# A new beginning for a two-block transformer kernel: modulation vectors, squares and the first block of weights before the norm

## The chip, the cores and the metric

The kernel runs on one core of a Trainium2 chip. The metric is the device time in microseconds of one execution. It is given as the median of three runs. Five engines work side by side and meet through semaphores: TensorE (PE) does matmuls into PSUM, VectorE (DVE) and ScalarE (ACT) work element by element, GpSimd (POOL) does so without access to PSUM, and SyncE (SP) issues most transfers.

## The reference, cut to what matters

The program computes two blocks one after the other, for 512 positions of 1024 features. The first has two layers of three sublayers (gated FFN, mixer, gated FFN), the second is another mixer with an FFN. The change touches the beginning of the first sublayer:

```python
c_act = jax.nn.silu(c)
for l in range(DEPTH):
    mod = (c_act @ w_mod[l] + b_mod[l]).reshape(c.shape[0], N_MOD, D_MODEL)
    h = modulate(x, g_norm[l, 0], mod[:, 0], mod[:, 1])     # shift, scale
    x = x + 0.5 * mod[:, 2][:, None, :] * swiglu(h, w_ffn1_gu[l], w_ffn1_down[l])
...
def rmsnorm(x, g):
    y = x * lax.rsqrt(jnp.mean(x * x, axis=-1, keepdims=True) + EPS)
    return y * g
def modulate(x, g, shift, scale):
    return rmsnorm(x, g) * (1.0 + scale[:, None, :]) + shift[:, None, :]
```

So h = rstd * (x * a) + shift with a = (1 + scale) * g, where rstd belongs to a position and a and shift to a feature. A product with weights W is then rstd * ((x * a) W) + shift W, and (x * a) W can be had before rstd is known.

## The kernel before, in words

Features lie on the 128 partitions, in 8 chunks, and the 512 positions on the free axis. All weights come as blocks of 1 MB (1024 x 256) into four places of `raw`. ScalarE rounds each half of a block to `w_hi` (line 1179), GpSimd takes the rest `w_lo` (line 464), two places each. A product of a chunk is three fp32r matmuls for each of two column tiles: high by high, low by high, high by low (lines 551 to 553). One block is therefore 8 x 2 x 3 = 48 matmuls over 512 columns. Blocks alternate between PSUM banks 0, 1 and 2, 3; `out_free` says when the pair of banks has been taken.

At the beginning SP issues `cond` (208 KB), three tables `mod_b`, `gains`, `ident` (104, 40 and 64 KB), then x (2048 KB), then the first four "positions", which are vectors of 512 modulation values with 2048 KB of weights each, in four pieces of 512 KB. Positions 0 and 1 make the shift, 2 and 3 the scale. Block 0 of the weights is issued ahead of position 3, block 1 behind it.

Two engines compute the positions. For 0 and 2 TensorE multiplies the activated condition, repeated over 128 columns in `cond_wide`, with the weights: 8 fp32 matmuls (line 859), of two passes each. VectorE then picks the diagonal (line 1721). For 1 and 3 VectorE multiplies and adds eight times over 512 columns (lines 2427 and 2429), copies the partial sums to `t_ring`, and TensorE sums the partitions by products with a column of ones (line 866). ScalarE squares x chunk by chunk (line 1185), VectorE adds the squares up (line 1729), and TensorE sums them over the partitions (lines 589, 600). VectorE makes the variance (1743), GpSimd the power (469), TensorE spreads rstd over the partitions (608). Then `norm` makes h chunk by chunk: VectorE x * a * rstd into PSUM (1837), ScalarE adds the shift and rounds (1216), VectorE takes the low part (1834). Block 0 starts with the first chunk of h.

All later sublayers begin in another way. `ahead` on ScalarE scales x by a alone (lines 1193, 1194), VectorE takes the low part (`scaled_x`, 1775), and TensorE multiplies the sublayer's first block with it (634 to 636) while the squares are still being summed. VectorE sums the shift's product with that block from `raw` (`bias_sum`), and `scale_part` (1811, 1815) multiplies the result by rstd afterwards. The order in each engine's queue is the order in which the code is written; no scheduler changes it.

## Time and profile before

| | us |
|---|---|
| median of 3 runs | 2747.59 |
| lowest and highest | 2746.55, 2747.94 |
| span of the profiled execution | 2745.7 |
| TensorE busy | 2682.1 (98%) |
| VectorE busy | 1357.7 (49%) |
| ScalarE busy | 1070.1 (39%) |
| GpSimd busy | 1142.1 (42%) |

The profiled execution's own time is its span, 2745.7 us, with 1.9 us less than the median of the runs. Busy shares are an average over the whole program; the change lies in the first 80 us, so the views of that stretch say more. Starts are counted in microseconds from the span's start. A matmul's duration overlaps that of the next one, so its cost is read from the distance of starts. A fp32 matmul has two passes and two rows in the trace; a fp32r matmul has one.

### The profile page before, as it was taken

Reading aid. Unit: us, or ns where it says so; the run is one execution under the profiler, and the core shown is the slowest. Engines: PE = TensorE matmul, PEld = TensorE weight load, DVE = VectorE, ACT = ScalarE, POOL = GpSimd, SP = SyncE. Lnnn points to the kernel's source line nnn. Section 1 sums busy time; section 2 is a strip of 40 time slices with the busy share of each in tenths; the row PEclk is TensorE's granted clock in tenths of the full one; section 3 lists DMA queues with packets and bytes.
Section 4 is the critical chain, followed back from the end, with each engine's and each line's share of the span. In section 5 each row is a group of like instructions: output and inputs, shape, how many; then the busy total and the mean of one; then the engine's idle time right before and its main releaser. Section 6 shows DMA issues by size and latency. Waiting matters only on the chain.

```text
span 2745.7 us, 34606 instructions
## 1 busy us (share of the span) xinstructions
PE 2682.1 (98%) x12784; PEld 2181.2 (79%) x12784; DVE 1357.7 (49%) x2212; ACT 1070.1 (39%) x1600; POOL 1142.1 (42%) x492
## 2 busy tenths in 40 slices
PE   6999999999999999999999999999999999999998
PEld 4888887788888888888778888888766878888886
DVE  5333247763232543324776333345764557674645
ACT  3222245452222532224545222246465563542333
POOL 2444444144444444444424444455321334344343
PEclk9999999999999999999999999999999999999999
DMA  7545432146454264543214545434310214322231
GB/s 285 198 160 201 160 138 92 47 144 215 163 204 164 100 215 161 199 162 138 92 47 145 210 166 201 167 123 161 110 47 32 77 70 169 108 99 100 92 108 46
DMA packets 70723, 378.82 MB, mean 138 GB/s; under 512 B 7936, under 2 KB 8704, under 8 KB 40352
## 3 DMA queue, kind: packets, MB, share of 16 engines
q1 hardware_dynamic: 65568, 358.56, 36.5%
q10 hardware_dynamic: 4992, 18.09, 1.8%
q8 instruction: 101, 1.65, 0.2%
q14 instruction: 62, 0.51, 0.1%
HBM read 368.23 MB, written 8.39 MB: 137 GB/s over the span
## 4 chain that ended last, share of the span: by engine, by line
PE 79%; DVE 10%; DVEq 4%; ACT 3%; issue 2%; DMA 1%; ACTq 1%; SPq 1%; POOL 0%
PE psum L551 21%; PE psum L553 21%; PE psum L552 21%; PE psum L570 1%; PE psum L572 1%; PE psum L571 1%; DVE psum L1837 1%; PE psum L730 1%; PE psum L732 1%; PE psum L731 1%; PE psum L665 1%; PE psum L664 1%; PE psum L663 1%; DVEq L2270 1%; DVE small L2051 1%
## 5 line engine op out<-in xcount | busy, mean ns | idle before, releaser
L464 POOL TENSOR_TENSOR w_lo<-raw,w_hi 128x1024 fp32r<-128x1024 f32 x464 | 1119.3, 2418 | 1484.3 <-ACT w_hi L1179 1469.4
L1179 ACT CAST w_hi<-raw 128x1024 fp32r<-128x1024 f32 x464 | 483.1, 1047 | 822.6 <-PE psum L553 696.5
L551 PE MATMUL psum<-h_hi,w_hi 128*128 128x512 f32 x1920 | 750.4, 391 | 8.9 <-DVE h_lo L1834 5.2
L553 PE MATMUL psum<-h_hi,w_lo 128*128 128x512 f32 x1920 | 748.0, 390 | 0.0
L552 PE MATMUL psum<-h_lo,w_hi 128*128 128x512 f32 x1920 | 748.0, 390 | 0.0
L551 PEld LDWEIGHTS psum<-h_hi,w_hi 128*128 128x128 f32 x1920 | 361.1, 188 | 87.7 <-issue 7.2
L553 PEld LDWEIGHTS psum<-h_hi,w_lo 128*128 128x128 f32 x1920 | 361.0, 188 | 75.3
L552 PEld LDWEIGHTS psum<-h_lo,w_hi 128*128 128x128 f32 x1920 | 361.1, 188 | 75.0 <-issue 0.5
L1920 DVE TENSOR_TENSOR psum<-act_ring,psum 128x512 f32<-128x512 f32 x85 | 59.2, 696 | 517.8 <-ACT act_ring L1249 517.4
L551 PE MATMUL psum<-hid_hi,w_hi 128*128 128x512 f32 x792 | 308.5, 389 | 0.8 <-DVEq L1869 0.8
L553 PE MATMUL psum<-hid_hi,w_lo 128*128 128x512 f32 x792 | 308.1, 389 | 0.0
L552 PE MATMUL psum<-hid_lo,w_hi 128*128 128x512 f32 x792 | 308.1, 389 | 0.0
L1865 DVE SCALAR_TENSOR_TENSOR x<-psum,gate,x 128x512 f32<-128x512 f32 x128 | 90.3, 747 | 334.6 <-PE psum L553 300.1
L1710 DVE CUSTOM_DVE_ANT_0 mod_sink<-mod_raw,psum 128x1024 f32<-128x1024 f32 x192 | 234.1, 1220 | 37.8 <-issue 26.7
L1249 ACT ACTIVATE act_ring<-psum 128x512 f32<-128x512 f32 x85 | 50.8, 598 | 355.1 <-PE psum L553 355.1
L551 PEld LDWEIGHTS psum<-hid_hi,w_hi 128*128 128x128 f32 x792 | 148.7, 188 | 32.7 <-issue 2.0
L553 PEld LDWEIGHTS psum<-hid_hi,w_lo 128*128 128x128 f32 x792 | 148.7, 188 | 30.9
L552 PEld LDWEIGHTS psum<-hid_lo,w_hi 128*128 128x128 f32 x792 | 148.7, 188 | 30.8
L2353 DVE SCALAR_TENSOR_TENSOR psum<-gpad,cpar,psum 128x441 f32<-128x441 f32 (+2 forms) x176 | 123.1, 699 | 14.0 <-issue 1.1
L570 PE MATMUL psum<-h_hi,w_hi 128*128 128x512 f32 x240 | 96.4, 401 | 0.0
L572 PE MATMUL psum<-h_hi,w_lo 128*128 128x512 f32 x240 | 93.7, 391 | 0.0
L571 PE MATMUL psum<-h_lo,w_hi 128*128 128x512 f32 x240 | 93.5, 390 | 0.0
(410 smaller groups left out, 3247.2 us busy)
## 6 DMA issues: line engine op xcount, KB each, us to landing
raw<-in_weights_dram SPq DMA_DIRECT2D x232, 1024.0 KB, 4.9
mod_raw<-in_mod_w_dram SPq DMA_DIRECT2D x192, 512.0 KB, 4.0
first_mods_a<-in_mod_w_dram SPq DMA_DIRECT2D x8, 512.0 KB, 11.1
first_mods_b<-in_mod_w_dram SPq DMA_DIRECT2D x8, 512.0 KB, 15.9
prod<-in_cond_rows_dram ACTq DMA_DIRECT2D x8, 512.0 KB, 3.5
first_mods_a<-gate_spill ACTq DMA_DIRECT2D x4, 1024.0 KB, 10.1
gate_spill<-gate_out_c ACTq DMA_DIRECT2D x5, 512.0 KB, 3.0
x<-in_xT_dram SPq DMA_DIRECT2D x1, 2048.0 KB, 7.9
```

The costliest lines, as they stand in the source:

```text
L464: pool.tensor_tensor(w_lo[:, k % 2, cs], raw[:, k % 4, cs], w_hi[:, k % 2, cs].bitcast(F32), ALU.subtract).then_inc(lo_ready, 1)
L551: pe.matmul(out, wh, rhs_hi[:, c, :], start=(c == ks[0]), stop=False)
L552: pe.matmul(out, wh, rhs_lo[:, c, :], start=False, stop=False)
L553: mm = pe.matmul(out, wl, rhs_hi[:, c, :], start=False, stop=(c == ks[-1]))
L570: pe.matmul(out, wh, rhs[0][:, c, :], start=(c == 0), stop=False)
L571: pe.matmul(out, wh, rhs[1][:, c, :], start=False, stop=False)
L572: mm = pe.matmul(out, wl, rhs[0][:, c, :], start=False, stop=(c == KC - 1))
L1179: act.copy(w_hi[:, k % 2, cs], raw[:, k % 4, cs]).then_inc(hi_ready, 1)
L1710: dve.tensor_tensor_reduce(mod_sink[:, :], mod_raw[:, piece % 2, :, :].rearrange("p k n -> p (k n)"), row_ps, 1.0, 0.0, ALU.mult, ALU.add, ...
L1865: o = dve.scalar_tensor_tensor(x[:, m, :], psum[:, 2 * (k % 2) + t, :], gate[:, m:m + 1], x[:, m, :], ALU.mult, ALU.add)
L1920: dve.tensor_tensor(ps, act_ring[:, j % 2, :], ps, ALU.mult).then_inc(prod_ready, 1)
L2353: dve.scalar_tensor_tensor(dst[:, rs, cs], src[:, rr, cc], tap(3 * (dy + 1) + dx + 1), dst[:, rs, cs], ALU.mult, ALU.add)
```

## The change

It gives the first sublayer the same form as the later ones and moves its work to TensorE. In words:

- SP issues position 2 first, then x, block 0, then positions 3, 0, 1 (`FIRST_ORDER`), into places of their own: two in `first_mods`, one in the `raw` places 2 and 3, one in `first_last` and `mod_raw`. Block 2 is issued after the third position's rows, the rest after the fourth's.
- All four positions are computed by TensorE with weights of 32 columns of which only the first is not zero. Matmul k goes to column group k mod 4 (`FIRST_TILE`). VectorE copies the bank and TensorE sums the partitions with ones.
- TensorE sums the squares of every chunk itself (`first_sums`); VectorE adds none.
- Block 0 is multiplied with x * a, chunk by chunk between these steps (`first_ahead`), and scaled by rstd inside `first_norm`. Block 1 is the first one that is multiplied with h.
- The shift's product with block 0 is 32 fp32r matmuls over two columns (`first_bias`): the shift's high and low part, with `w_hi` and `w_lo`.
- The counters of the later sublayers move up by one (3 * l becomes 3 * l + 1, and so on).

```diff
+FIRST_ORDER = (2, 3, 0, 1)
+FIRST_TILE = 32
...
-            for pos in range(FIRST_MODS):
-                if pos == FIRST_MODS - 1:
+            for n, pos in enumerate(FIRST_ORDER):
+                for piece in range(MOD_PIECES):
+                    sp.dma_start(first_piece(n, piece), a["mod_w"][pos, piece]).then_inc(first_landed[n][piece // (MOD_PIECES - 1)], 16)
+                if n == 0:
+                    sp.dma_start(x[:, :, :].rearrange("p c n -> p (c n)"), a["xT"]).then_inc(x_landed, 16)
                     load_block(0, 0)
...
+            sp.wait_ge(msum_ready, 3)
             load_block(0, 2)
+            sp.wait_ge(msum_ready, 4)
...
+            splits(0, 0, 1)
             rms(0)
-            splits(0, 0, 1)
...
-                    mm = pe.matmul(psum[:, pos, :], cond_wide[:, k, :], first_mod(pos)[:, k, :], start=(k == 0), stop=(k == DC - 1))
+                    r = FIRST_TILE * (k % 4)
+                    at = k % MOD_K * MOD_COLS
+                    mm = pe.matmul(first_bank(n)[r:r + FIRST_TILE, :], cond_wide[:, k, :], first_piece(n, k // MOD_K)[:, at:at + MOD_COLS],
+                                   start=(k < 4), stop=(k >= 4))
...
+            def first_ahead():
+                pe.wait_ge(wide_ready, 1)
+                first_rows(0)
+                first_columns(0)
+                first_sums(range(4))
+                wait_block(0, 0, 0)
+                pe.wait_ge(out_free[0], 1)
+                first_chunk(0)
+                first_rows(1)
+                first_chunk(1)
+                first_columns(1)
+                first_chunk(2)
+                first_chunk(3)
+                first_sums(range(4, DC))
+                wait_block(0, 0)
+                first_chunk(4)
+                rms_rows(0)
+                first_rows(2)
+                first_chunk(5)
+                first_columns(2)
+                first_rows(3)
+                first_chunk(6)
+                first_columns(3)
+                first_chunk(7)
+                first_bias()
...
+            first_squares(range(4))
+            act.wait_ge(first_a_ready, 1)
+            scaled_chunks(0, (0, 1), h_hi)
+            split_hi(0, 0, (0,))
+            scaled_chunks(0, (2,), h_hi)
+            split_hi(0, 0, (1,))
+            scaled_chunks(0, (3,), h_hi)
+            first_squares(range(4, DC))
+            ahead(0, range(4, DC))
+            split_hi(0, 1)
...
+            scaled_x(0, range(4))
+            first_copy(1)
+            first_take(1)
+            first_factors(1)
+            dve.drain().then_inc(ssq_ready, 1)
+            dve.drain().then_inc(sq_used, 3)
+            rms(0)
+            scaled_x(0, (4,))
+            first_copy(2)
+            scaled_x(0, (5,))
+            first_take(2)
+            first_copy(3)
+            scaled_x(0, (6, 7))
+            first_take(3)
...
+                for c in range(DC):
+                    chunk(c)
+                    if c:
+                        lo(c - 1)
+                    if c == 5:
+                        dve.wait_ge(block_done, 3)
+                        dve.tensor_reduce(bias_col, psum[:, S_BANK, 4:8].rearrange("p (t e) -> p t e", e=2), AX.X, ALU.add)
+                        scale_part(0, 0, 0, 0)
                     dve.drain()
+                lo(DC - 1)
+                scale_part(0, 0, 0, 1)
```

How the change stands in the queues: on VectorE of the kernel before, from its multiply-adds for the fourth position (`first_mods_b`, taken in at line 2427) to the first chunk of the norm:

```order
L2427 TENSOR_SCALAR psum<-first_mods_b,cond 128x512 [waits first_landed3_0]
L2429 SCALAR_TENSOR_TENSOR psum<-first_mods_b,cond,psum 128x512 x5
L2429 SCALAR_TENSOR_TENSOR psum<-first_mods_b,cond,psum 128x512 [waits first_landed3_1]
L2429 SCALAR_TENSOR_TENSOR psum<-first_mods_b,cond,psum 128x512
L2431 COPY t_ring<-psum 128x512
```

VectorE of the changed kernel, from the variance (line 1827 there) to the first chunk of the norm (line 2556); `h_lo<-psum,h_hi` is the low part of a scaled chunk, `t_ring<-psum` the copy of a position:

```order
L1827 TENSOR_SCALAR var<-psum 128x4 [waits cols_ready]
L1858 TENSOR_TENSOR h_lo<-psum,h_hi 128x512 [waits xa_hi_ready]
L2506 COPY t_ring<-psum 128x512 [waits msum_ready]
L1858 TENSOR_TENSOR h_lo<-psum,h_hi 128x512 [waits xa_hi_ready]
L2513 TENSOR_TENSOR mods<-psum,mod_b 128x4 [waits first_cols]
L2506 COPY t_ring<-psum 128x512 [waits msum_ready]
L1858 TENSOR_TENSOR h_lo<-psum,h_hi 128x512 [waits xa_hi_ready] x2
L2513 TENSOR_TENSOR mods<-psum,mod_b 128x4 [waits first_cols]
L2544 COPY shift<-mods 128x8
L2547 CAST shift<-shift 128x8
L2549 TENSOR_TENSOR shift<-shift 128x8
L2556 SCALAR_TENSOR_TENSOR psum<-x,a_col,psum 128x512 [waits rb_ready]
```

The multiply-adds are gone, and the low parts of the scaled chunks stand between copies that wait for TensorE.

TensorE of the kernel before, from the second position it computes itself to block 0:

```order
L859 MATMUL psum<-first_mods_b,cond_wide 128x512 [waits first_landed2_0]
L859 MATMUL psum<-first_mods_b,cond_wide 128x512 x5
L859 MATMUL psum<-first_mods_b,cond_wide 128x512 [waits first_landed2_1]
L859 MATMUL psum<-first_mods_b,cond_wide 128x512
L866 MATMUL psum<-ones,t_ring 128x1 [waits first_part]
L866 MATMUL psum<-ones,t_ring 128x1 x3
L551 MATMUL psum<-h_hi,w_hi 128x512 [waits h_ready,out_free0,lo_ready]
```

TensorE of the changed kernel, from the third position's rows through chunk 5 of block 0 to the fourth position's rows:

```order
L880 MATMUL psum<-raw,cond_wide 32x512 [waits first_landed2_1]
L880 MATMUL psum<-raw,cond_wide 32x512
L906 MATMUL psum<-h_hi,w_hi 128x512 [waits xa_ready]
L907 MATMUL psum<-h_lo,w_hi 128x512
L908 MATMUL psum<-h_hi,w_lo 128x512
L906 MATMUL psum<-h_hi,w_hi 128x512
L907 MATMUL psum<-h_lo,w_hi 128x512
L908 MATMUL psum<-h_hi,w_lo 128x512
L888 MATMUL psum<-ones,t_ring 128x1 [waits first_part]
L888 MATMUL psum<-ones,t_ring 128x1 x3
L880 MATMUL psum<-first_last,cond_wide 32x512 [waits first_landed3_0,first_took]
```

The rows of a position now write 32 partitions each, and products of block 0 stand between the positions.

## Rows read from the trace of the kernel before

**Rows 1.** The page, chain that ended last, shares by engine:
```profile
PE 79%; DVE 10%; DVEq 4%; ACT 3%; issue 2%; DMA 1%; ACTq 1%; SPq 1%; POOL 0%
```
**Rows 2.** Waits of TensorE, whole run: line, releaser, us in total, times, longest:
```profile
PE psum L551 <- DVE h_lo L1834: 5.2, 3, 4.6
PE psum L891 <- DVEq L2169: 3.8, 4, 1.0
```
**Rows 3.** Timeline of TensorE: start us, us, engine, line, operation, operands, count:
```profile
45.24 0.76 PE L551 MATMUL psum<-h_hi,w_hi 128*128 128x512 f32 x1 [4.62 <-DVE h_lo L1834]
...
50.49 0.47 PE L551 MATMUL psum<-h_hi,w_hi 128*128 128x512 f32 x1
...
69.62 0.39 PE L551 MATMUL psum<-h_hi,w_hi 128*128 128x512 f32 x1
```
**Rows 4.** Chain of waits over the first 80 us: start us, us, what:
```profile
15.63 16.50 DMA first_mods_b<-in_mod_w_dram
32.16 0.76 DVE psum L2427
...
42.40 0.77 DVE psum L1837
```
**Rows 5.** DMA issues: transfer, queue, count, KB each, median us to landing:
```profile
raw<-in_weights_dram SPq DMA_DIRECT2D x232, 1024.0 KB, 4.9
...
x<-in_xT_dram SPq DMA_DIRECT2D x1, 2048.0 KB, 7.9
```
**Rows 6.** Timeline of TensorE and VectorE, small operations of the first 45 us:
```profile
24.90 1.03 PE L600 MATMUL psum<-ones,sq 128*128 128x1 f32 x8
...
26.86 0.80 PE L866 MATMUL psum<-ones,t_ring 128*128 128x1 f32 x3 [0.93 <-DVEq L2432]
...
28.59 1.09 PE L608 MATMUL psum<-ident,rstd 128*128 128x128 f32 x4
...
40.82 0.16 DVE L1724 TENSOR_TENSOR mods<-psum,mod_b 128x4 f32<-128x4 f32 x1
41.05 0.16 DVE L2437 TENSOR_TENSOR mods<-psum,mod_b 128x4 f32<-128x4 f32 x1
```
**Rows 7.** Timeline of TensorE, two column groups of 64, then the full width:
```profile
2034.43 0.27 PE L1096 MATMUL psum<-prod,vals 128*64 128x128 f32 x1
...
2034.54 0.27 PE L1096 MATMUL psum<-prod,vals 128*64 128x128 f32 x1
2034.55 0.27 PE L1096 MATMUL psum<-turned_b,vals 128*64 128x128 f32 x1
2034.75 0.88 PE L1082 MATMUL psum<-ident,mprobs 128*128 128x128 f32 x6
```
**Rows 8.** Stretches: us, PE, PEld, DVE, ACT, POOL busy (x), granted clock, DMA, GB/s:
```profile
14.40:19.60 5.20, 5.17 (x6) 2.18 (x7) 2.68 (x5) 2.29 (x4) 0.00 (x0) 1.00 1.03 414
19.90:24.00 4.10, 4.10 (x10) 1.80 (x10) 3.71 (x6) 0.00 (x0) 0.00 (x0) 1.00 1.03 411
24.10:26.70 2.60, 1.83 (x17) 1.75 (x15) 2.38 (x4) 0.00 (x0) 0.00 (x0) 1.00 1.06 436
26.80:33.50 6.70, 6.64 (x17) 4.30 (x18) 2.92 (x13) 1.99 (x2) 5.07 (x3) 0.50 1.02 410
...
40.60:45.20 4.60, 0.02 (x1) 0.00 (x0) 3.70 (x11) 1.27 (x2) 1.39 (x1) 0.85 1.03 419
45.20:50.50 5.30, 5.26 (x13) 4.13 (x14) 5.02 (x8) 2.08 (x4) 0.00 (x0) 0.50 0.50 203
```
**Rows 9.** Groups of ScalarE from 384 to 430 us: count, busy us, mean ns:
```profile
L1179 ACT CAST w_hi<-raw 128x1024 fp32r<-128x1024 f32 x7 | 7.2, 1048 | 5.9 <-PE psum L553 5.1 <-DVE psum L1837 0.8
...
L1193 ACT ACTIVATE psum<-x,a_col 128x512 f32<-128x512 f32 x8 | 5.4, 672 | 0.0
```
**Rows 10.** Timeline of GpSimd, the split of block 0:
```profile
29.45 4.65 POOL L464 TENSOR_TENSOR w_lo<-raw,w_hi 128x1024 fp32r<-128x1024 f32 x2 [1.29 <-ACT w_hi L1179]
```
**Rows 11.** Timeline of VectorE, end of the first normalisation:
```profile
53.36 1.60 DVE L1834 SCALAR_TENSOR_TENSOR h_lo<-psum,shift,h_hi 128x512 fp32r<-128x512 f32 x2
```
**Rows 12.** Timeline of VectorE, copy of the row factors in a later stage:
```profile
422.87 0.68 DVE L1811 COPY ssq<-psum 128x512 f32<-128x512 f32 x1
```

More of the change, by code:

```diff
@@ L867, in first_columns, with first_sums @@
                                    skip_group_check=True)
-                mm.then_inc(msum_ready, 1)
-            pe.wait_ge(wide_ready, 1)
-            first_rows(0)
-            x_cols(0, 0)
-            first_columns(1)
-            rms_rows(0)
-            first_rows(2)
-            first_columns(3)
+                mm.then_inc(first_cols, 1)
+            def first_sums(cs):
+                for c in cs:
+                    pe.wait_ge(sq_ready, c + 1)
+                    for t in range(T // P):
+                        mm = pe.matmul(psum[:, S_BANK, t:t + 1], sq[:, c % 2, t * P:(t + 1) * P], ones[:, 0:1], start=(c == 0 and t == 0),
+                                       stop=(c == DC - 1), skip_group_check=True)
+                    mm.then_inc(cols_ready if c == DC - 1 else first_sq_used, 1)
@@ new lines, in first_chunk @@
+            def first_chunk(c):
+                pe.wait_ge(xa_ready, c + 1)
+                for t in range(2):
+                    wh, wl = (w[:, 0, c * 256 + t * P:c * 256 + (t + 1) * P] for w in (w_hi, w_lo))
+                    pe.matmul(psum[:, t, :], wh, h_hi[:, c, :], start=(c == 0), stop=False)
+                    pe.matmul(psum[:, t, :], wh, h_lo[:, c, :], start=False, stop=False)
+                    mm = pe.matmul(psum[:, t, :], wl, h_hi[:, c, :], start=False, stop=(c == KC - 1))
+                if KC // 2 <= c < KC - 1:
+                    mm.then_inc(xa_used, 1)
@@ new lines, in first_bias @@
+            def first_bias():
+                pe.wait_ge(shift_split, 1)
+                for c in range(KC):
+                    for t in range(2):
+                        for w in (w_hi, w_lo):
+                            mm = pe.matmul(psum[:, S_BANK, 4 + 2 * t:6 + 2 * t], w[:, 0, c * 256 + t * P:c * 256 + (t + 1) * P], shift2[:, c, :],
+                                           start=False, stop=(c == KC - 1), skip_group_check=True)
+                    if c == KC // 2 - 1:
+                        mm.then_inc(front_done, 1)
+                mm.then_inc(block_done, 1)
@@ L1189, in ahead, with scaled_chunks @@
                 act.wait_ge(a_ready, i + 1)
+                scaled_chunks(i, chunks, xa_hi)
+            def scaled_chunks(i, chunks, xa_hi):
                 for m in chunks:
@@ L1298, in mixer @@
             def mixer(l, g, k0, n):
[L1299 removed]
+                first = (3 * l + 1, g, k0)
                 norm(n, first=first)
@@ L1830, in norm, with norm_chunks @@
                 dve.wait_ge(rb_ready, summed(n if r is None else r))
+                norm_chunks(n, first)
+            def norm_chunks(n, first):
                 def lo(c):
@@ L2411, in _, with first_copy @@
             dve.tensor_copy(ones_r[:, :], ones[:, :])
-            for k in range(DC):
-                dve.tensor_scalar(cond_wide[:, k, :], ones[:, :], cond[:, k:k + 1], None, ALU.mult)
+            dve.memset(cond_wide[:, :, :], 0.0)
+            dve.drain()
+            dve.tensor_copy(cond_wide[:, :, 0:1], cond[:, 0:DC].rearrange("p (c o) -> p c o", o=1))
             dve.drain().then_inc(wide_ready, 1)
+            def first_copy(n):
+                dve.wait_ge(msum_ready, n + 1)
+                dve.tensor_copy(t_ring[:, n % 2, :], first_bank(n))
+                dve.drain().then_inc(first_part, 1)
@@ new lines, in _ @@
+            first_copy(1)
[11 more added lines that the diff above has]
+            first_take(3)
+            dve.tensor_copy(shift[:, :], mods[:, 0:8])
+            dve.drain()
+            shift_col = shift[:, :].rearrange("p (c o) -> p c o", o=1)
@@ new lines, in _, with first_norm, chunk, lo @@
+            dve.tensor_copy(shift2[:, 0:DC, 0:1], shift_col)
+            dve.drain()
+            dve.tensor_tensor(shift2[:, 0:DC, 1:2], shift_col, shift2[:, 0:DC, 0:1].bitcast(F32), ALU.subtract)
+            dve.drain().then_inc(shift_split, 1)
+            dve.drain().then_inc(bias_ready, 1)
+            def first_norm():
+                def chunk(c):
+                    dve.scalar_tensor_tensor(t_ps(c), x[:, c, :], a_col[:, c:c + 1], psum[:, S_BANK + 1, :],
+                                             ALU.mult, ALU.mult).then_inc(t_ready, 1)
+                def lo(c):
+                    dve.wait_ge(h_hi_ready, c + 1)
+                    dve.scalar_tensor_tensor(h_lo[:, c, :], t_ps(c), shift[:, c:c + 1], h_hi[:, c, :].bitcast(F32),
+                                             ALU.add, ALU.subtract).then_inc(h_ready, 1)
+                for c in range(DC):
[6 more added lines that the diff above has]
+                        scale_part(0, 0, 0, 0)
+                    dve.drain()
+                lo(DC - 1)
+                scale_part(0, 0, 0, 1)
```

147 lines of the change are left out of this document (70 added, 77 removed).

## The prediction, made before the changed kernel ran

> **What bounds the kernel now.** I read the chain's shares on the page first: 79% of the chain that ended last is TensorE's [rows 1]. TensorE's waits over the whole run come next. Its line 551 waited 5.2 us for VectorE in three places, 4.6 of it before the very first product [rows 2, 3]; the next cause after that holds 3.8 us in all, in pieces of at most 1.0. So what is won or lost before the steady stream of products begins should reach the end nearly whole, and I price only the beginning. The mark I use is the first matmul of the third block of weights (block 2), because from there on the two programs do the same work. In the kernel before, block 0 starts at 45.24, its first 12 matmuls take until 50.49, 0.44 us each, and from 50.49 on they are 0.228 apart (84 of them to 69.62). 36 more of block 0 and 48 of block 1 are these 84, so block 2 begins at 69.6 [rows 3].
>
> What holds the start back? The chain of waits over the first 80 us says: 16.5 us of transfer until 32.16, then VectorE's eight multiply-adds of 0.76 us for the fourth modulation vector, its copy, the sums over the diagonal, the factors, and the normalisation of chunk 0 [rows 4]. After that TensorE runs block 0 and then block 1, and the normalisation only has to keep ahead of it.
>
> **Transfers.** x is issued at 2.60 and lands 7.9 us later, at 10.5, with 2.52 MB moved (2048 KB and four tables of 416 KB). Until 32.16 three whole modulation vectors of 2048 KB, block 0 of 1024 KB and three pieces of 512 KB came on top, 11.44 MB in all. That is 8.92 MB in 21.66 us, 0.412 MB/us [rows 4, 5]. The change reorders the same bytes: modulation 2, x, block 0, modulation 3, 0, 1, block 1. At this rate modulation 2 is whole at 10.6 (its first three pieces at 9.3), x at 15.7, block 0 at 18.2, modulations 3, 0, 1 at 23.3, 28.3, 33.4, block 1 at 36. The last modulation lands when it did. Transfers give nothing and take nothing; they only allow work to start earlier.
>
> **Prices on TensorE.** Passes over 512 columns in fp32 took 0.86 us each in the first stretch of them (6 in 5.17) and 0.43 from 19.7 on, with 10 starts in the 4.1 us after 19.9 [rows 8]. The first stretch shows a granted clock of 1.00, but its passes have the low clock's pace; the record begins later than they do. A modulation vector is 16 such passes. Now four passes stand in four column groups of 32. Line 1096 shows two groups of 64 working together: passes over 128 columns in pairs that start 0.01 us apart, each pair 0.11 after the last [rows 7]. Four groups were never tried here; the bounds are four abreast (1.7 us high, 3.4 low) and no overlap at all (6.8 and 13.7). I take four abreast, as the pairs of line 1096 lose nothing. A column or square sum is 8 passes over one column, 0.9 us in total at the high clock (8 in 1.03, with the last one's tail of 0.14) and 0.21 apart, 1.7 us, at the low one (3 in 0.80, with a tail) [rows 6]. One chunk of block 0, 6 matmuls, is 1.36 or 2.56 us.
>
> The Trainium skill, "TensorE: Matmul & The Clock Gate", section "Part 3: Packing small matmuls — row/col tiling", gives 2.38 times for three column groups, which is 0.79 of the ideal. By that estimate the four groups would cost 2.2 us and the sum below would be 1.4 us longer; the trace's pairs show no such loss. The Trainium skill, "TensorEngine Tiling (Array Packing)", section "Key Properties", says that a change of tiling mode drains the engine. The trace agrees in kind, and sizes it: the next full-width matmul stands 0.20 us after the last narrow pass instead of 0.11 [rows 7], so eight switches would add 0.7 us.
>
> **TensorE's clock.** The granted clock is 0.50, the low level, from 26.8 to 33.5 and from 45.2 to 50.5, after a stretch of one-column passes (24.1 to 26.7) and after idleness (40.6 to 45.2) [rows 8]. The new beginning contains both kinds of stretch: almost nothing from 13 to 26 us, and then four square sums in a row. I therefore count the low clock for the early sums, chunk 0 and most of the rows after it, and again for chunk 4 and some of what follows.
>
> **The change step by step**, in the time of the trace of before.
> (a) Removed on VectorE: 16 multiply-adds, 6 additions of squares and 8 diagonal sums, of which the stretch from 32.16 to 42.40, 10.2 us, was on the path.
> (b) First modulation on TensorE at 9.3, copy, column sums, factors: ready near 15.7, behind the transfer of x. Costs nothing.
> (c) x lands at 15.7. ScalarE squares chunks 0 and 1, but has two places only: squares 2 and 3 wait for TensorE's sums. At 1.7 us a sum they end at 20.6. Two scaled chunks, 4 x 0.61 = 2.4, a cast of 1.0 and GpSimd's 2.4 [rows 9, 10] give 26.5 for chunk 0 of block 0. Block 0 landed 8 us before.
> (d) chunk 0 at 2.6, the rows of modulation 3 at 3.0, chunk 1, column sums, chunks 2 and 3: 1.4 + 0.9 + 2.7. That is 37.1.
> (e) Four square sums, 3.6, then variance and the scaled chunk 4 on VectorE before TensorE may go on, 1.2: 41.9.
> (f) chunk 4 low 2.6, the row transposes 0.8 (4 in 1.09 at the low clock, tail included [rows 6]), the rows of modulation 0 half low 2.0: 47.3.
> (g) VectorE's copy stands ahead of its chunk 5 in the queue, so TensorE waits for both, 0.8 + 0.9; then chunk 5 and column sums 2.3: 51.3. Rows of modulation 1, 1.7, and again copy plus chunk 6, 1.8: 54.8. chunk 6 and column sums 2.3: 57.1.
> (h) Taking the sums and splitting the shift is five small VectorE instructions of 0.16, 0.24 apart with their drains [rows 6]: 58.3. Call this S; it was 42.40.
> (i) chunk 7 and the 32 narrow products for the shift run beside the normalisation. No row has such a product. Bounds: nothing, or 32 x 0.11 = 3.6 us (6.8 low). The first normalised chunk takes 2.8 us anyway (42.40 to 45.24 [rows 3, 4]) and VectorE sets the pace afterwards, so even 6.8 costs at most 0.5. I take nothing.
> (j) The normalisation took 12.6 us, from 42.40 to the end of its last line 1834 at 54.96 [rows 11]. Now VectorE also copies the row factors and scales the first half of block 0 inside it: 0.75 + 0.8, as in the later stage whose copy takes 0.68 [rows 12], and a reduction of 0.24. Chunks 6 and 7 of block 1 come 1.8 us later, at S + 14.3. Block 2 needs block 0's banks: second scaling 0.8, gate product 0.8, ScalarE's cast 0.7, low part 0.8, thus S + 17.5. This is a new wait; before, block 0 had long been taken.
> (k) SP now waits for sums before it issues block 2's raw weights, near 47.5. They land some 5 us later [rows 5] and ScalarE casts them at about S + 6.7 = 65. Block 3 and the next modulation pieces queue behind that wait, with more room still. No cost.
>
> Sum: block 2 at 58.3 + 17.5 = 75.8 against 69.6, **6.2 us later**. The block-0 products (13.4 us) did go beside the transfers. What eats it is that TensorE became a serial queue of small steps between 26.5 and S, with VectorE and ScalarE in turn. The profiled span is 2745.7 and the median 2747.59, 1.9 us more; a shift of the start moves both alike: 2747.6 + 6.2 = **2753.8 us**. Break-even is S = 52.1.
>
> **Rivals.** *The clock stays high.* TensorE does get work more evenly than before. Then sums are 0.9 each, chunk 0 starts near 24, chunk 4 and all rows are high; S comes to about 52.5 and block 2 to 70.0: 2748.0. Against it speaks the fall after 24.1 to 26.7. *The groups overlap by pairs only.* Line 1096 has no more than two. Then each rows step is 1.7 us longer high and more low; S near 64, 2759.5. With no overlap at all, 6.8 each, S passes 75: 2771. *Faster: the waits between engines close up.* TensorE's own work from 24 to S at the high clock is 8 x 1.36 + 3 x 1.7 + 3 x 0.9 + 4 x 0.9 + 0.8 = 23.1 us. If VectorE's chunks 5 and 6 stand ready whenever TensorE asks, S is 48.4 and block 2 starts at 65.9, 3.7 earlier: 2744. It decides at S = 52.1, that is when all waits and low-clock losses after 24 us together are under 3.7 us. For it: the data is there by 33.4. Against it: the queue order puts each copy ahead of the chunk.
>
> **How the numbers follow.** Forecast (four abreast, low clock twice) 0.45, with an own range of 2751 to 2757; clock high 0.2; pairs 0.2; waits closed 0.1; no overlap 0.05. The range leaves out the last two and little more: 2746.5 to 2762. A measurement of this kernel tells about 0.2%, 5.5 us, from no change: slower means above 2753.1. Of the forecast's 0.45 some 0.3 lies above that and 0.15 below. Slower: 0.3 + 0.2 + 0.05 = 0.55; same: 0.15 + 0.2 = 0.35; faster 0.1.
>
> **What would show it.** In the timeline of the changed kernel: line 880's passes, 16 in about 1.7 or 3.4 us, or in twice that; chunk 0 of block 0 (line 906) near 26.5; a granted clock of 0.50 around 27 to 30 and around 41 to 46; TensorE idle before chunks 5 and 6 with VectorE's line 1858 as releaser; line 2556 first at about 58; block 2's first line 568 matmul about 17.5 us behind it, released by VectorE. The prediction is wrong if line 2556 starts before 52, if the rows passes overlap differently, or if the stream after block 2 has idle times that the kernel before has not.

## The result: 2754.6 us, 0.25% slower than before

| | before | after |
|---|---|---|
| median, lowest to highest, 12 runs each, us | 2747.90 (2746.55 to 2748.72) | 2754.56 (2753.03 to 2755.96) |
| span of the profiled execution, us | 2745.7 | 2752.4 |
| first normalised chunk on VectorE (S) | 42.40 | 58.09 |
| first matmul of block 2 | 69.62 | 75.56 |

The ratio is 1.0025, with a 95% interval of 1.0017 to 1.0032. The forecast was 2753.8. TensorE's waits in the first 85 us, after the change (line, releaser, us in total, times, longest):

```profile
PE psum L880 <- DMA first_mods<-in_mod_w_dram: 9.3, 1, 9.3
PE psum L906 <- DVE h_lo L1858: 4.4, 3, 1.6
PE psum L906 <- POOL w_lo L481: 3.1, 1, 3.1
PE psum L568 <- DVEq L2017: 0.9, 1, 0.9
PE psum L888 <- DVEq L2507: 0.8, 1, 0.8
```

The single wait of 4.6 us for the normalisation [rows 2] is gone. Four new ones, 7.5 us in all, stand before chunks 0, 4, 5 and 6 of block 0 (line 906), and one of 0.9 before block 2, the new wait for block 0's banks. The timeline of TensorE after the change shows where they lie (start us, us, engine, line, operation, operands, count, in brackets the idle time before and what ended it):

```profile
16.04 6.99 PE L897 MATMUL psum<-ones,sq 128*128 128x1 f32 x32 [0.40 <-ACT sq L1776]
26.15 0.80 PE L906 MATMUL psum<-h_hi,w_hi 128*128 128x512 f32 x1 [3.12 <-POOL w_lo L481]
...
29.01 2.81 PE L880 MATMUL psum<-first_mods,cond_wide 128*32 128x512 f32 x16
...
36.90 3.63 PE L897 MATMUL psum<-ones,sq 128*128 128x1 f32 x32
41.70 0.76 PE L906 MATMUL psum<-h_hi,w_hi 128*128 128x512 f32 x1 [1.18 <-DVE h_lo L1858]
...
44.40 0.65 PE L625 MATMUL psum<-ident,rstd 128*128 128x128 f32 x4
44.98 1.93 PE L880 MATMUL psum<-raw,cond_wide 128*32 128x512 f32 x16
48.52 0.50 PE L906 MATMUL psum<-h_hi,w_hi 128*128 128x512 f32 x1 [1.62 <-DVE h_lo L1858]
...
54.44 0.50 PE L906 MATMUL psum<-h_hi,w_hi 128*128 128x512 f32 x1 [1.63 <-DVE h_lo L1858]
...
58.23 0.17 PE L918 MATMUL psum<-shift,w_hi 128*128 128x2 f32 x1
...
61.65 0.35 PE L918 MATMUL psum<-shift,w_lo 128*128 128x2 f32 x1
61.87 0.77 PE L568 MATMUL psum<-h_hi,w_hi 128*128 128x512 f32 x1
...
75.56 0.47 PE L568 MATMUL psum<-h_hi,w_hi 128*128 128x512 f32 x1 [0.87 <-DVEq L2017]
```

Here one reads both halves of the story. The work of block 0 does lie beside the transfers: chunk 0 starts at 26.15, 19.1 us before the 45.24 of [rows 3]. But TensorE's steps then follow each other until 58.2, and S, which was 42.40 [rows 4], is 58.09. The matmul of block 2 at 75.56 answers to the one at 69.62. Block 2 follows S after 17.5 us instead of 27.2, 9.75 less, because block 0 is already done, but S comes 15.7 later; that leaves 5.9.

VectorE after the change, from the copy of the third position to the last product before block 2:

```profile
46.97 0.69 DVE L2506 COPY t_ring<-psum 128x512 f32<-128x512 f32 x1 [5.42 <-PE psum L880]
47.78 0.69 DVE L1858 TENSOR_TENSOR h_lo<-psum,h_hi 128x512 fp32r<-128x512 f32 x1
...
58.09 1.61 DVE L2556 SCALAR_TENSOR_TENSOR psum<-x,a_col,psum 128x512 f32<-128x512 f32 x2 [0.22 <-issue]
...
67.09 0.68 DVE L1894 COPY ssq<-psum 128x512 f32<-128x512 f32 x1
67.84 0.70 DVE L1898 TENSOR_TENSOR psum<-psum,ssq 128x512 f32<-128x512 f32 x1
...
70.88 1.60 DVE L2561 SCALAR_TENSOR_TENSOR h_lo<-psum,shift,h_hi 128x512 fp32r<-128x512 f32 x2
72.39 0.69 DVE L1898 TENSOR_TENSOR psum<-psum,ssq 128x512 f32<-128x512 f32 x1
73.27 0.76 DVE L2004 SCALAR_TENSOR_TENSOR psum<-psum,cond_now,act_ring 128x512 f32<-128x512 f32 x1 [0.19 <-issue]
74.68 0.69 DVE L2015 TENSOR_TENSOR hid_lo<-psum,hid_hi 128x512 fp32r<-128x512 f32 x1 [0.65 <-ACT hid_hi L1337]
```

The first two rows are the wait before chunk 5: the rows of the position end, VectorE copies (46.97 to 47.66), only then takes the low part (47.78 to 48.47), and TensorE goes on at 48.52. The last rows are the chain from S to block 2, 17.47 us long.

Between block 2 and the end the two programs differ little: 2745.7 - 69.6 = 2676.1 us before, 2752.4 - 75.6 = 2676.8 after. So 5.9 of the 6.7 us lie ahead of block 2. The other 0.7 is no more than this remainder varies between the kernels below (2674.8 to 2677.9).

### The profile page after: what moved, and what is told of

The parts are those of the page before. It is cut to its first block, busy times and chain, and to the rows that moved or that the text cites. A ratio compares the mean times of both kernels' runs of the same rounds, so it can differ in the third digit from the quotient of the medians.

```text
span 2752.4 us, 34844 instructions
## 1 busy us (share of the span) xinstructions
PE 2691.1 (98%) x12912; PEld 2190.7 (80%) x12912; DVE 1347.4 (49%) x2186; ACT 1079.7 (39%) x1616; POOL 1141.4 (41%) x492
## 4 chain that ended last, share of the span: by engine, by line
PE 79%; DVE 10%; DVEq 4%; ACT 3%; issue 2%; ACTq 1%; DMA 1%; POOL 1%; SPq 0%
PE psum L568 21%; PE psum L569 21%; PE psum L570 21%; PE psum L587 1%; PE psum L589 1%; PE psum L588 1%; DVE psum L1923 1%; PE psum L747 1%; PE psum L749 1%; PE psum L748 1%; PE psum L682 1%; PE psum L681 1%; PE psum L680 1%; DVEq L2356 1%; DVE small L2137 1%
## 6 DMA issues: line engine op xcount, KB each, us to landing
x<-in_xT_dram SPq DMA_DIRECT2D x1, 2048.0 KB, 10.8
```

## The experiments

My theory: TensorE's serial queue of small steps, with VectorE in turn, sets S, and block 2 follows S by a fixed chain of VectorE. The rivals: the groups overlap less than I took; the clock is what costs; the narrow products for the shift hold back block 1. All medians were taken beside runs of the kernel before, whose median was 2747.4 to 2747.8 in each set.

| kernel | median us | ratio to before, interval | S | block 2 | span |
|---|---|---|---|---|---|
| two_groups | 2761.40 | 1.0050, 1.0033 to 1.0067 | 65.33 | 82.80 | 2760.7 |
| one_group | 2773.10 | 1.0095, 1.0078 to 1.0112 | 76.74 | 94.22 | 2771.0 |
| chunks_first | 2751.22 | 1.0014, 1.0004 to 1.0023 | 55.43 | 72.91 | 2749.4 |
| sums_spread | 2752.87 | 1.0022, 1.0013 to 1.0032 | 56.26 | 73.73 | 2749.7 |
| filled | 2756.91 | 1.0035, 1.0022 to 1.0048 | 61.79 | 79.26 | 2755.6 |
| all_three | 2755.60 | 1.0026, 1.0013 to 1.0039 | 59.93 | 77.40 | 2754.1 |
| moved | 2748.34 | 1.0003, 0.9994 to 1.0012 | 56.45 | 73.93 | 2751.2 |
| two_shift_chunks | 2755.77 | 1.0030, 1.0019 to 1.0041 | 59.57 | 77.05 | 2754.5 |
| old_order_groups | 2745.74 | 0.9995, 0.9986 to 1.0004 | 40.59 | 67.67 | 2742.6 |
| old_order_groups_filled | 2745.11 | 0.9989, 0.9980 to 0.9998 | 42.64 | 68.94 | 2744.2 |
| groups_split_later | 2744.01 | 0.9987, 0.9978 to 0.9996 | 41.32 | 67.92 | 2743.4 |
| groups_rows_first | 2742.52 | 0.9982, 0.9973 to 0.9991 | 37.38 | 63.80 | 2738.6 |

S, block 2 and span are those of the one profiled execution. It can lie anywhere in its set: for sums_spread it is the fastest of ten, for moved and groups_split_later the longest of eleven. two_groups and one_group have 4 executions each, filled 5, all_three 6, two_shift_chunks 7, the other kernels 10 or 11.

### How many column groups work abreast

```diff
-FIRST_TILE = 32
+FIRST_TILE = 64     # two_groups; 128 in one_group
...
-                    r = FIRST_TILE * (k % 4)
+                    r = FIRST_TILE * (k % (P // FIRST_TILE))
```

(`start` and `stop` move with the number of groups.)

> The changed kernel with the position weights in two column groups of 64 instead of four of 32 (matmul k in group k mod 2). Theory (all four groups work at once): a position's rows take twice as long, 3.4 us instead of 1.9 at the high clock; two of them are on the path behind chunk 0 at the high clock and one partly at the low one, so the norm (58.09 in the changed kernel) starts 5 to 6 us later, near 63.5, and the median is near 2760. Rival (the four groups only overlap by neighbours, so four bring nothing over two): rows stay 1.9 to 2.7 us and the time is that of the changed kernel, 2754.6.

> The changed kernel with full-width position weights, one group of 128. Theory: 16 passes one behind the other, 6.8 us a position at the high clock, 5 us more each for two positions and 5 to 8 for the first one behind chunk 0; less where the clock is now high all along: norm at 72 to 76, median 2768 to 2773. Rival (rows are not on the path, TensorE only waits elsewhere): under 4 us more than the changed kernel.

The rows of the last position in the kernel two_groups and then in one_group (timeline of TensorE; the last four of the sixteen passes stand under another tile name, since their weights lie in `mod_raw`):

```profile
56.42 2.79 PE L880 MATMUL psum<-first_last,cond_wide 128*64 128x512 f32 x12
59.05 1.03 PE L880 MATMUL psum<-mod_raw,cond_wide 128*64 128x512 f32 x4
```

```profile
64.36 5.40 PE L880 MATMUL psum<-first_last,cond_wide 128*128 128x512 f32 x12
69.59 1.88 PE L880 MATMUL psum<-mod_raw,cond_wide 128*128 128x512 f32 x4
```

From the first start to the last end that is 7.1 us with one group, 3.7 with two, and 1.9 with four (50.90 to 52.82 in the changed kernel; 44.98 1.93 in its timeline above). These times include the tail of the last passes, so four groups overlap without a loss that shows. S comes 7.2 and 18.7 us later than in the changed kernel, and the median follows with 6.8 and 18.5.

### The order of the queue

chunks_first moves chunks 4 and 5 ahead of the copy of the third position on VectorE, and chunk 6 ahead of that of the fourth:

```diff
-            scaled_x(0, (4,))
+            scaled_x(0, (4, 5))
             first_copy(2)
-            scaled_x(0, (5,))
+            scaled_x(0, (6,))
             first_take(2)
             first_copy(3)
-            scaled_x(0, (6, 7))
+            scaled_x(0, (7,))
```

> The changed kernel with two moves in VectorE's queue: the low part of chunk 5 ahead of the third position's copy, that of chunk 6 ahead of the fourth's. Theory (the queue order makes TensorE wait): the idle times of 1.6 us before chunk 5 and 1.7 before chunk 6 go, the norm starts 3.3 us earlier, near 54.8, and the median is near 2751.3. Rival (other waits take their place, the column sums then wait for the copy): under 1 us gained.

TensorE's waits there, first 85 us:

```profile
PE psum L906 <- POOL w_lo L481: 3.1, 1, 3.1
PE psum L897 <- ACT sq L1776: 1.5, 1, 1.5
PE psum L906 <- DVE h_lo L1858: 1.2, 1, 1.2
```

The waits for VectorE fell from 4.4 us in three places to 1.2 in one, 3.2 less, and the median fell by 3.3. S came only 2.66 us earlier in the profile, where the low clock lasted longer: the third position's rows took 2.77 us instead of 1.93. These waits had been on the path, as the prediction's step (g) said.

sums_spread puts the four square sums one by one between the steps:

```diff
                 first_chunk(1)
+                first_sums((4,))
                 first_columns(1)
+                first_sums((5,))
                 first_chunk(2)
+                first_sums((6,))
                 first_chunk(3)
-                first_sums(range(4, DC))
+                first_sums((7,))
```

> The changed kernel with the square sums of chunks 4 to 7 placed one by one between chunks 1, 2 and 3 of block 0 instead of in a row behind them. Theory (the run of one-column passes lets the clock fall): no low stretch from 41.1 to 44.5, chunk 4 takes 1.4 instead of 2.9 us, and the norm starts 1.5 to 2.5 us earlier, median near 2752.5. Rival (the clock falls anyway, or the fall is from the 1.2 us wait before chunk 4): the low stretch stays and the time is that of the changed kernel within 0.5 us.

Stretches of the kernel sums_spread (us, then busy us and count of PE, PEld, DVE, ACT, POOL, then granted clock, DMA share, GB/s), and of the changed kernel:

```profile
41.00:46.00 5.00, 3.92 (x26) 1.95 (x26) 0.75 (x2) 1.34 (x2) 0.26 (x1) 1.00 0.00 0
```

```profile
41.70:44.40 2.70, 2.70 (x7) 2.01 (x8) 0.00 (x0) 1.38 (x3) 0.12 (x1) 0.50 0.00 0
```

In the changed kernel chunk 4 follows 32 one-column passes in a row, and the granted clock is 0.50 for it, the level of 1.2 GHz. In the profile of sums_spread it stays at 1.00. Chunk 4's wait of 1.18 us is unchanged. From chunk 4 to the third position's rows it is 2.00 us (41.14 to 43.14) instead of 3.28 (41.70 to 44.98). So the low clock cost 1.3 us there, about what step (f) charged. The other 0.56 us of the 1.83 by which S came earlier lies ahead of chunk 4 and is not the edit's: chunk 0 already started 0.75 earlier (25.40). The median came 1.7 us earlier.

That spreading the passes keeps the clock up is not shown for every execution. Two of the ten took 2756.8 and 2757.7 us, longer than any of the changed kernel, and in the profile of moved, below, the sums are spread too and chunk 4 has the low pace.

moved has both orders, and VectorE takes chunk 4's low part before it makes the variance:

```diff
-            rms(0)
             scaled_x(0, (4,))
+            rms(0)
+            scaled_x(0, (5,))
```

> The changed kernel with the orders of chunks_first and of sums_spread together: the square sums of chunks 4 to 7 stand one by one between the steps, chunks 4, 5 and 6 go before the copy that they were behind, and VectorE takes the low part of chunk 4 before it makes the variance. No fill. Theory (each order removes a different wait): chunks_first gained 2.7 us in the start of the normalisation (58.09 to 55.43) and sums_spread 1.8 (to 56.26); together 53.6 or earlier, median 2754.6 - 4.5 = 2750 or less. Rival (they take away the same waits, or the clock falls again): start 55 to 56, median 2751 to 2752.5.

The median of 11 runs is 2748.34, 6.2 us less than the changed kernel and level with the kernel before. The two gains, 3.3 and 1.7, add. The 1.2 us beyond them is the size of the wait before chunk 4, which is gone in moved; no kernel has that move alone. The profile fell on the longest of the eleven executions (2752.97), so its S of 56.45 is not the usual one. It is of use for another reason:

```profile
37.00:46.80 9.80, 9.80 (x37) 8.10 (x39) 1.55 (x3) 5.68 (x9) 1.46 (x2) 0.50 0.01 3
```

TensorE was busy without a gap there, and was still granted 0.50 for 9.8 us. The mean granted clock and span of the eleven runs go in three bunches: 0.995 with 2745.4 to 2746.5 (six), 0.997 with 2747.4 to 2747.5 (three), 0.992 with 2750.9 and 2751.2 (two). So executions of the same program differ by 5 us. Where the clock fell in the others is not recorded, and what decides it stays open.

### Matmuls that only keep TensorE at work

filled puts 28 fp32r matmuls over 128 columns, whose result nobody reads, between the fourth square sum and chunk 0:

```diff
+            def filler(n):
+                for _ in range(n):
+                    pe.matmul(psum[:, S_BANK + 1, 0:P], ones_r[:, :], ones_r[:, :], start=True, stop=True)
+
             def first_ahead():
...
                 first_sums(range(4))
+                filler(28)
                 wait_block(0, 0, 0)
```

> The changed kernel with 28 matmuls over 128 columns that compute nothing needed, between the fourth square sum and chunk 0 of block 0, where TensorE waits 3.1 us for GpSimd's split. Theory (the low clock from 26.15 on comes from the idleness before): chunk 0 and the rows behind it run at the high clock, 2 us sooner, median near 2752.5. Rival (3 us of fill come too late, since the stretch of sums before them already holds the clock low): the low stretch stays to about 30.8 and the time changes by under 0.5 us.

Timeline of TensorE in filled:

```profile
23.39 6.21 PE L926 MATMUL psum<-ones_r 128*128 128x128 f32 x28
29.41 0.73 PE L906 MATMUL psum<-h_hi,w_hi 128*128 128x512 f32 x1
...
32.20 3.14 PE L880 MATMUL psum<-first_mods,cond_wide 128*32 128x512 f32 x16
```

The fill took 6.0 us instead of the 3 that were idle, 0.21 apart, and chunk 0 behind it still had the low pace (0.43 apart). The theory failed: the fill did not raise the clock. The rival had the low pace right but not the price, since it said under 0.5 us: the fill itself stood in the way, chunk 0 came 3.3 us later (0.5 of it because the first rows started later in this profile), and the median rose by 2.4. all_three has this fill and the orders of moved:

> The changed kernel with the moves of chunks_first, the sums of sums_spread and the fill of filled together, and VectorE's low part of chunk 4 ahead of the variance. Theory: the gains add, 3.3 + 2 + 1 + up to 2: norm at 50 to 51.5, block 2 near 68, median 2746.5 to 2748, about the kernel before. Rival (the serial queue of TensorE has its own length): norm not below 53, median 2750 or more.

Its chunk 0 was late too, and the granted clock was 0.50 again from 40.5 to 50.5:

```profile
22.00:30.00 8.00, 8.00 (x38) 8.00 (x39) 2.77 (x4) 6.95 (x11) 4.71 (x2) 0.50 1.03 410
...
40.50:50.50 10.00, 10.00 (x37) 8.05 (x39) 1.55 (x3) 5.93 (x9) 1.71 (x2) 0.50 0.00 0
```

Its median is 7.3 us above that of moved, which lacks only the fill. Chunk 0 came 3.5 us later in the profiles (29.74 against 26.19); the rest is not explained. (One of its six executions took 8938.88 us; nothing in the profile, which is of another, explains it.)

### The narrow products for the shift

```diff
-                for c in range(KC):
+                for c in (0, KC - 1):
                     for t in range(2):
                         for w in (w_hi, w_lo):
...
-                    if c == KC // 2 - 1:
+                    if c == 0:
                         mm.then_inc(front_done, 1)
```

> The changed kernel with the shift's product with block 0 taken over two of its eight chunks only: 8 narrow products instead of 32; what it leaves out is the contribution of the other six chunks. Theory of the prediction's step (i), the narrow products are hidden: block 1 starts when its first chunk of h is ready, about 61.2 to 61.9 either way, block 2 at 75.6 as in the changed kernel, median 2754.6 within 0.5. Rival (they hold back block 1, which started 0.2 us after the last of them): block 1 starts 1 us or more earlier and block 2 follows, 2753.5 or less.

TensorE in two_shift_chunks:

```profile
60.39 0.25 PE L918 MATMUL psum<-shift,w_lo 128*128 128x2 f32 x1
62.42 0.47 PE L568 MATMUL psum<-h_hi,w_hi 128*128 128x512 f32 x1 [1.78 <-DVE h_lo L2561]
...
77.05 0.47 PE L568 MATMUL psum<-h_hi,w_hi 128*128 128x512 f32 x1 [0.88 <-DVEq L2017]
```

With 8 products instead of 32, block 1 starts 2.85 us after S (59.57) instead of 3.78 (58.09 to 61.87). The rival was right in that. But block 2 starts 17.48 after S, against 17.47: nothing of it reaches the end. The median did not fall either; it is 1.2 us higher, and in the profile S itself is 1.5 later, ahead of the edit. Chunk 4 was already 1.2 late there: the first rows could start 0.52 us later (9.82 against 9.30, when their weights had landed), and the second position's rows took 3.48 us instead of 2.81, with more of them at the low pace. That is one execution; why this program's median is higher stays open.

### Only the positions, in the order of before

Does any part of the change pay by itself? old_order_groups is the kernel before with all four positions on TensorE in four column groups, and VectorE's 16 multiply-adds and 8 diagonal sums gone:

```diff
-                    mm = pe.matmul(psum[:, pos, :], cond_wide[:, k, :], first_mod(pos)[:, k, :], start=(k == 0), stop=(k == DC - 1))
+                    r = 32 * (k % 4)
+                    mm = pe.matmul(psum[r:r + 32, pos, :], cond_wide[:, k, :], first_mod(pos)[:, k, :], start=(k < 4), stop=(k >= 4))
...
             x_cols(0, 0)
-            first_columns(1)
+            first_columns(0)
+            first_rows(1)
             rms_rows(0)
+            first_columns(1)
             first_rows(2)
+            first_columns(2)
+            first_rows(3)
             first_columns(3)
```

> The kernel before with one part of the change alone: all four positions by TensorE in four column groups, VectorE's 16 multiply-adds and the diagonals gone; transfers, squares, the norm before block 0 as they were. Theory (the chain from 32.16 to 42.40 was the path): the last piece lands near 33.4, the rest of the rows, copy, column sums and factors take 3.5, the norm starts near 37 instead of 42.40 and the median falls by 5.4 to 2742.5. Rival (block 0 then runs longer at the low clock, or waits for GpSimd's split): only 2 to 3 us gained.

It gained 1.6 us, not 5.4, and its interval does not leave 1.0 out. VectorE, then GpSimd there:

```profile
38.33 2.17 DVE L1760 TENSOR_TENSOR a_col<-a_col,gains 128x8 f32<-128x8 f32 x1
40.59 1.60 DVE L1843 SCALAR_TENSOR_TENSOR psum<-x,a_col,psum 128x512 f32<-128x512 f32 x2
```

```profile
38.14 4.64 POOL L465 TENSOR_TENSOR w_lo<-raw,w_hi 128x1024 fp32r<-128x1024 f32 x2 [2.97 <-ACT w_hi L1185]
```

A product of 128 x 8 numbers took 2.17 us where its neighbours take 0.17. It ended at 40.50. GpSimd's two halves take 2.34 each, so the first ended at 40.48. The profile of old_order_groups_filled, below, has the same: 2.17 us again, from 40.38 to 42.55, while GpSimd's second half ended at 42.53. The kernel before has a smaller case of it that I had not seen:

```profile
41.29 0.72 DVE L1751 COPY shift<-mods 128x8 f32<-128x8 f32 x1
```

That copy ended at 42.01, and GpSimd's split of the same block ran from 37.33 for 4.66 us, to 41.99. groups_split_later tests the cause: GpSimd begins that split only after the first normalised chunk.

```diff
             splits(0, 0, 1)
+            pool.wait_ge(t_ready, 1)
```

> The kernel of old_order_groups, and GpSimd begins its split of block 1 only when VectorE has written the first normalised chunk. In old_order_groups VectorE's small product for a_col (line 1760, 128x8) took 2.17 us, from 38.33 to 40.50, and ended with GpSimd's running split (38.14 to 40.48). Theory (a small VectorE operation waits for the whole GpSimd instruction that has begun before it): the a_col product takes 0.17 us, the first normalised chunk starts at 38.4 instead of 40.59, median 2745.7 - 2.2 = 2743.5. Rival (the product is slow for another reason, or the normalisation beside the split is slower by as much): a_col still near 2 us, or 2745.7 again.

```profile
40.50 0.16 DVE L2437 TENSOR_TENSOR mods<-psum,mod_b 128x4 f32<-128x4 f32 x1 [1.17 <-PE psum L869]
...
41.07 0.17 DVE L1761 TENSOR_TENSOR a_col<-a_col,gains 128x8 f32<-128x8 f32 x1
41.32 1.60 DVE L1844 SCALAR_TENSOR_TENSOR psum<-x,a_col,psum 128x512 f32<-128x512 f32 x2
```

The product is back at 0.17. From the last sum to S it is 0.82 us, where old_order_groups had 2.82 (37.77 to 40.59). The median is 1.7 us lower, 2744.01; the two were run in different sets, and the intervals of their ratios overlap, so the size of the gain is less sure than the stall's end. (S itself is later than in the other profile, because TensorE was at the low pace for longer: the third position's rows took 3.46 us instead of 1.92. This profile is of the longest of the eleven executions.) The Trainium skill, "SBUF — State Buffer", section "SBUF: two separate sides", says that a VectorE operation with two SBUF inputs and a GpSimd operation that reads SBUF lock each other out for a whole instruction, whoever starts first. The trace agrees: the product with two inputs in SBUF waited for 2.17 us, and the normalisation of x behind it, whose third operand is in PSUM, ran at 0.8 beside the second half.

groups_rows_first also lets TensorE make the fourth position's rows before the third's column sums:

```diff
             first_rows(2)
-            first_columns(2)
             first_rows(3)
+            first_columns(2)
             first_columns(3)
```

(On VectorE the two copies stand before the two sums.)

> The kernel of groups_split_later, and TensorE makes the rows of the fourth position before it sums the columns of the third, so that VectorE's copies follow each other. Theory (what is left ahead of the normalisation is the chain copy, columns, rows, copy, columns): the fourth position's rows start near 32.2, when three of its pieces have landed, wait once for the last piece and end near 34.3 instead of 35.8; normalisation from about 36.9, median about 2742.0. Rival (the transfer sets it: the fourth position's last piece lands later than 34): start of the normalisation 37.5 or later, median 2742.7 to 2743.5.

Both the theory and its rival were near: S was 37.38, between their 36.9 and 37.5. The chain of waits there (start us, us, what) and TensorE's timeline:

```profile
15.75 16.52 DMA first_mods_b<-in_mod_w_dram
32.27 0.04 issue
32.31 2.32 PE psum L862 x16
34.64 1.89 PE psum L869 x16
```

```profile
40.22 0.77 PE L553 MATMUL psum<-h_hi,w_hi 128*128 128x512 f32 x1 [3.70 <-DVE h_lo L1841]
```

Block 0 starts 5.0 us before the 45.24 of [rows 3], and the median is 5.1 us below that of before. The interval of the ratio, 0.9973 to 0.9991, leaves 1.0 out: this kernel beats both. As in the kernel before, the transfer of the fourth position stands on the chain, but from there to S it is 5.1 us (32.27 to 37.38) instead of 10.2 (32.16 to 42.40 [rows 4]).

old_order_groups_filled adds to old_order_groups twelve 512-column matmuls without use ahead of block 0, which runs at the low clock (12 matmuls of 0.43, as in [rows 3]):

```diff
             first_columns(3)
+            wait_block(0, 0, 0)
+            pe.wait_ge(first_part, 4)
+            for _ in range(12):
+                pe.matmul(psum[:, 0, :], ones_r[:, :], w_hi[:, 0, 0:T], start=True, stop=True)
```

> As old_order_groups, with 12 matmuls over 512 columns that compute nothing needed, between the last column sums and block 0. Theory (idleness before block 0 costs its low clock, 12 matmuls at 0.43 instead of 0.23, 2.5 us): block 0 starts at the high clock, another 2 to 2.5 us earlier, median near 2740.3. Rival (the clock has fallen before the fill, so the fill itself is slow and delays block 0): no gain or up to 2 us slower than old_order_groups.

```profile
39.11 4.49 PE L886 MATMUL psum<-w_hi,ones_r 128*128 128x512 f32 x12
45.48 0.56 PE L552 MATMUL psum<-h_hi,w_hi 128*128 128x512 f32 x1 [1.88 <-DVE h_lo L1844]
```

The median moved by 0.6 us, within the intervals. The clock rose within the fill, whose mean granted clock is 0.64 (39.10 to 43.60), but the fill ended 1.9 us before block 0, and block 0's products 2 to 8 stand 0.43 apart again. The eleven executions reach from 2739.84 to 2746.60, wider than those of old_order_groups (2744.32 to 2747.50), and the profile is of a long one (2746.00); what the fill did in the short ones is not shown. Whether a fill that reaches up to block 0 would help wasn't tried.

## Why the prediction was right, point by point

| step | predicted | measured |
|---|---|---|
| (b) first rows on TensorE | 9.3 | 9.30 |
| (c) chunk 0 | 26.5 | 26.15 |
| (d) chunk 3 done | 37.1 | 36.90 |
| (e) chunk 4 | 41.9 | 41.70 |
| (f) third position's rows done | 47.3 | 46.91 |
| (g) column sums done; chunk 6; column sums done | 51.3; 54.8; 57.1 | 50.90; 54.44; 56.75 |
| (h) S | 58.3 | 58.09 |
| (j) block 2 | 75.8 | 75.56 |
| median | 2753.8 | 2754.56 |

The agreement is finer than the profiles repeat: the first rows start at 9.30 here, and between 9.26 and 10.14 in the variants, before any of their edits. So the mechanism and the sizes are borne out to some tenths of a microsecond, and the last digit is luck.

Bounds and transfers: x landed 10.8 us after its issue at 4.50, at 15.3, where 15.7 was predicted. That the transfers neither give nor take held.

Column groups: four abreast was the choice between unequal bounds, from pairs alone [rows 7]. The two kernels with wider groups showed that the sizes of the two rivals with less overlap were nearly right as well (predicted 2759.5 and 2771, measured 2761.4 and 2773.1). The estimate by the ratio that the Trainium skill, "TensorE: Matmul & The Clock Gate", section "Part 3: Packing small matmuls — row/col tiling", gives for three groups, 1.4 us longer, did not come out: S was 0.2 us earlier than the sum without it.

Step (c): the sum was right, and its parts nearly. GpSimd's split (23.74, 2.36 us) released chunk 0 as said. The 3.1 us of idleness before it were not won back by the fill that was tried.

Clock: by the pace, low for the early sums, chunk 0 and most rows of the second position (2.8 us for 16 passes), low again for chunk 4. The sign that I had named for it, a granted clock of 0.50 around 27 to 30, did not show: the changed kernel's profile has 1.00 from 16.0 to 36.9. But chunk 0's products stand 0.43 apart, as chunk 4's do where the profile has 0.50, and the profile of sums_spread has 0.50 for the same chunk 0 (25.4 to 28.2). Around 41 to 46 the sign came only in part, 0.50 until 44.4 and 1.00 from 45.0. There step (f) was a little off: I charged the third position's rows with 2.0 us and called that half low, though by my own prices, 1.7 and 3.4, half low is 2.55. The rows ran at the high pace (1.93 with their tail). So the two slips cancelled, which was luck; in chunks_first the same rows took 2.77. The transposes, charged with 0.8, took 0.6. With the 0.2 that chunk 4 came earlier that is the 0.4 us by which (f) was too long. A third low stretch, 61.8 to 65.0 on block 1, I had not named. It is harmless, because VectorE sets that pace: block 2 came 17.47 to 17.48 us after S in every variant of the changed kernel, wherever the clock fell.

Step (g): the waits before chunks 5 and 6 are shown by chunks_first to be real and on the path. Step (i): shown by two_shift_chunks; the narrow products cost 3.4 us of TensorE, delay block 1 by 0.9 and the end by nothing. Step (j): shown by the constant 17.47. It is the dearest single term, since in the kernel before block 2 came 27.2 us after S but with 96 matmuls in between, and now with 48. With TensorE's work of block 0 done by about S (its last product starts at 58.00), a free stream would have put block 2 near S + 14; the wait for banks and VectorE's scaling took the rest. That split of the term is worked out, not tested.

Step (k) held: but for chunk 0's, no wait of TensorE for weights stands in the first 85 us.

The faster rival, waits that close up, needed S below 52.1. Its sum was wrong in one term: it counts 8 x 1.36 for chunks, but chunk 7 runs behind S, so its S would be 47.0 and not 48.4, and the median 2742.5. It failed in the changed kernel partly for the reason given, the place of the copies in VectorE's queue: moved, with nothing but other orders, has no wait of TensorE between chunk 0 and S in its profile, and its median came to 2748.3, level with before. But that is not 2744 either. In that profile the low clock stands in place of the waits (37.0 to 46.8), and S is 56.45.

What the prediction left unseen is outside its sum: that VectorE's small operations ahead of S can wait for GpSimd, and that the positions in column groups, the only part of the change that was tried in the old order, bring something there: 1.6 us alone, not clear of noise, and 3.6 and 5.1 with GpSimd's split moved and then the rows moved too, both clear of it. Whether another part would pay alone was not tried.

## What to carry to other kernels

Work that is moved beside a transfer is won only if the engine that does it has nothing else to do before the point that releases the rest; here TensorE took over block 0 ahead of the normalisation, and the start of the normalisation moved back by 15.7 us, more than the 13.4 us of work that was brought forward. Price such a change by the date of that point, step by step through the queue, and look in each queue for a copy that stands ahead of what another engine is waiting for. Where a few tiny operations stand on the path, see what GpSimd is doing at that moment.

## What the runs showed of the hardware that I had not expected

- A VectorE product of 128 x 8 with both inputs in SBUF took 2.17 us instead of 0.17 while a GpSimd subtraction of 128 x 1024 ran, and ended with it; it took 2.17 us again in a second kernel, and 0.17 in two kernels with the subtraction moved.
- Sixteen fp32 passes over 512 columns took 1.9 us in four column groups, 3.7 in two, 7.1 in one, tails included: no loss that shows at four.
- Twenty-eight fp32r matmuls over 128 columns stood 0.21 us apart and left the next product at 0.43, the low pace; nor did twelve over 512 columns, followed by 1.9 us of idleness, keep block 0 at the high one.
- TensorE busy without a gap from 37.0 to 46.8 us was granted 0.50 throughout in one execution of a kernel whose median is 4.6 us shorter. all_three's profile has such a stretch too, from 40.5 to 50.5.
- The granted clock of a profile's beginning can read 1.00 where the pace is low: 26.1 to 29.0 in the changed kernel, with products 0.43 us apart.
- fp32r products over two columns start 0.11 us apart at the high clock, as one-column fp32 passes do (58.23 to 61.65 for 32).
